# A diffusion layer with expert choice on one core: roots in batches and a new tail order, a column-tiled router, and the first attention unit moved into the gap

## The chip, the cores and the metric

One Trainium2 chip, one core of it. The metric is the device time of one launch in microseconds. The kernel before took 947.57 us, the median of three runs (947.54, 947.57, 952.59).

## The reference

One layer over 128 context tokens and 512 latent tokens of width 1024, all in float32. The attention sublayer has two groups of eight query heads with two key/value heads each (head size 64): group A global with normed and rotated queries and keys, group B windowed with a learned sink. Latents read their own keys and 128 cached context keys. Then comes a mixture of 16 experts by expert choice.

```python
def ffn_sublayer(x, shift, scale, gate, g_pre_ffn, ...):
    h = modulate(x, g_pre_ffn, shift, scale)           # rms_norm(x, g) * (1 + scale) + shift
    return x + gate * rms_norm(expert_choice_moe(h, ...), g_post_ffn)

def expert_choice_moe(h, w_router, w_gate, w_up, w_down):
    cap = 2 * T // 16                                  # 64 latent rows, 16 context rows per expert
    aff = softmax(einsum('btd,de->bte', h, w_router))
    g, idx = top_k(swapaxes(aff, 1, 2), cap)
    xg = h[idx]                                        # per expert
    y = (silu(xg @ w_gate) * (xg @ w_up)) @ w_down * g
    return zeros.at[idx].add(y)                        # for context and latents apart
```

Both kinds of token pass the same layer with their own modulation vectors. Outputs are both streams and the context's new keys and values.

## The kernel before, in words

The program is written out by hand for each engine, in its queue's order, with semaphores between engines. Tokens lie in five tiles of 128 (`TILES`): tile 0 is context, tiles 1 to 4 are latents.

**Projections.** `project(i)`, i = 0 to 14, makes columns for the five tiles three times (keys and values, then A's queries, then B's). ScalarE copies each result (`nat`), VectorE norms and rotates it (`rot`), TensorE turns it (`turn_qk(k)` is the tile of i = k - 1), ScalarE copies the high part (`high_part(k)`) and VectorE subtracts for the low part (`low_part(k)`). `rotate_last` and `turn_qk(15)` belong to the last tile, i = 14, and run among the first attention units.

**Attention.** 80 units (`HEAD_UNITS`) of one head and one tile, 40 of group A and then 40 of group B (`A_UNITS` = 40). Unit u passes `scores(u)` on TensorE, `maxima(u)` on VectorE (maximum and factor), `exponentials(u)` on ScalarE, normalisation on VectorE, `turn_probs(u)` on TensorE, `copy_pT(u)` on ScalarE, and for each pair `values` on TensorE and `attn_out` on VectorE. In iteration u TensorE does `turn_probs(u - 1)`, `scores(u + 2)`, values, and for B also the output projection of a tile that is ready, spread over the eight units of the next one. Behind it come, still inside the loop, the norm (roots on POOL), the residual `add_out`, the turn of x1 (`turn_x1`), and `route_logits(o)`: eight matmuls whose stationary side is the token tile and whose moving side is 16 columns of the router table `wrm`. `logits_of`, `exp_logits` and `affinities` make the softmax over experts. Tiles 3 and 4 are finished behind the loop, and VectorE selects rows for all experts (`top_eight`).

**Experts.** Eight slots of 2 MB hold weights; SP issues each load when its slot is free. Slots 0 to 5 are loaded for expert 0 when attention's buffers are free, slots 6 and 7 (over `reg2_qt`) with expert 1's gate weights when the normed rows are stored. POOL gathers rows by indirect DMA and scatters results by indirect DMA with addition. `product_c` is one slot's product for the context rows, `product_l` for the latents; both split the array in column groups of 32. `turn_rows_c`, `turn_rows_l` turn gathered rows; `keep_busy` issues matmuls whose result nobody reads. Expert 0 begins with its context products in front of `gate_l(0, 0)`, from where each expert follows the last.

**The end.** The sums over all experts but the last are read back and squared on ScalarE, gated (`gate_sum`), rooted on POOL (`root` is a power by -0.5) and added to x1 (`add_x1`), while the last expert still runs. Its rows are made apart: `add_last(n)` (n = 1 context, 0 latents), a squared sum over ScalarE, a matmul that merges partitions (line 1091, behind all expert products on TensorE), `mean_last`, a root, and `rows_last_c` in four parts or `rows_last_l`. POOL stores these rows by two indirect DMAs, the first behind the stores of all five tiles:

```python
            pool.wait_ge(stored, 16 * (4 + TILES))
            pool.wait_ge(f_ready, TILES + 4)
```

## Time and profile before

| | |
|---|---|
| time of the profiled execution | 948.19 us |
| its span, first to last instruction | 946.2 us |
| median of the three runs | 947.57 us |
| TensorE busy | 884.3 us (93%) |
| VectorE / ScalarE / POOL busy | 365.8 / 216.5 / 102.6 us |
| mean granted TensorE clock | 0.986 of full |
| moved by DMA | 269.31 MB, 285 GB/s over the span |

The page cuts the span into 40 slices of 23.7 us. Its DMA row stands at 9 in the first slices, falls to 0 during attention and is at 9 from slice 17 to the last but one; the row of TensorE is at 9 nearly throughout, so the shares of the whole span tell little. A timeline row gives the start, the time from its first to its last instruction, engine, line, operation, shapes, and in brackets the idle time before it with what ended it. A float32 matmul leaves two records, so 8 matmuls are x16. Windows give busy us of each engine in a stretch, with the number of instructions in brackets, the granted clock as a share of 2.4 GHz, DMA's share and its rate.

### The profile page before, as it was taken

To read this page: it belongs to the slowest core of one execution; us is meant where nothing else is said; L and a number is where in the kernel's file an instruction comes from. 1 tells how busy PE (TensorE), PEld (TensorE's weight loads), DVE (VectorE), ACT (ScalarE), POOL (GpSimd) and SP (SyncE) were. 2 spreads that over 40 slices of the span, in tenths; PEclk is the share of its full clock that TensorE was granted. 3 is DMA by queue.
4 is the path that set the end of the run, shared out by engine and by line. 5 is a ranking of instruction groups with operands and counts; after the bars stand their busy time and mean duration, and the time that the engine had idled before them with its cause. 6 is when DMAs were issued, how large, how long until landed. Compare 5 with 4: busy or idle time off the path is not lost. (4 is left out here: it accounts for less than half of the span.)

```text
span 946.2 us, 19909 instructions
## 1 busy us (share of the span) xinstructions
PE 884.3 (93%) x8641; PEld 442.2 (47%) x8641; DVE 365.8 (39%) x977; ACT 216.5 (23%) x528; POOL 102.6 (11%) x137
## 2 busy tenths in 40 slices
PE   3999998899899999779999999999999999999984
PEld 3544444777656665533444443443444443433431
DVE  4255635888766766811112021121113120210126
ACT  3132223666645653400000000000000000000012
POOL 2021200000000000100110111011101101110225
PEclk9999999999999999899999999999999999999998
DMA  9997532300001116969999999999999999999983
GB/s 337 351 367 279 212 144 96 122 2 1 2 1 46 45 46 239 414 242 405 398 396 411 397 398 403 404 397 397 411 397 397 396 410 398 398 407 391 359 321 151
DMA packets 77717, 269.31 MB, mean 285 GB/s; under 512 B 6208, under 2 KB 9984, under 8 KB 77632
## 3 DMA queue, kind: packets, MB, share of 16 engines
q1 hardware_dynamic: 72384, 251.42, 67.8%
q0 software_dynamic: 4160, 13.90, 5.1%
q10 hardware_dynamic: 1088, 2.74, 0.7%
q8 instruction: 68, 1.11, 0.5%
q14 instruction: 17, 0.14, 0.0%
HBM read 252.06 MB, written 15.99 MB: 283 GB/s over the span
## 5 line engine op out<-in xcount | busy, mean ns | idle before, releaser
L954 PE MATMUL ps<-ring,reg 128*32 128x512 f32 x1792 | 201.6, 592 | 0.0
L1812 DVE TENSOR_SCALAR mod<-ps,kt 64x512 f32<-64x512 f32 x30 | 22.5, 750 | 255.9 <-PE ps L954 255.7
L954 PEld LDWEIGHTS ps<-ring,reg 128*32 128x32 f32 x1792 | 59.1, 110 | 111.8 <-issue 103.3
L966 PE MATMUL ps<-ring,values_in 128*32 128x256 f32 x1536 | 93.6, 386 | 4.0 <-issue 2.9
L1325 ACT ACTIVATE reg<-ps 128x256 f32<-128x256 f32 x16 | 6.1, 384 | 366.6 <-PE ps L1006 354.1
L954 PE MATMUL ps<-ring,kt 128*32 128x512 f32 x768 | 86.8, 592 | 0.0
L809 PE MATMUL ps<-ring,reg 128*128 128x512 f32 x160 | 76.4, 604 | 0.0
L966 PEld LDWEIGHTS ps<-ring,values_in 128*32 128x32 f32 x1536 | 50.0, 112 | 54.1 <-issue 24.8
L655 PE MATMUL ps<-ring,reg_qt 128*128 128x512 f32 x160 | 70.6, 594 | 0.0
L966 PE MATMUL ps<-ring,reg 128*32 128x256 f32 x1024 | 60.9, 379 | 2.5 <-DMA ring<-in_w_down 1.9
L1269 ACT ACTIVATE ring<-ps 128x640 f32<-128x640 f32 (+3 forms) x80 | 44.4, 555 | 72.5 <-PE ps L738 69.9
L738 PE MATMUL ps<-ident,ring 128*128 128x128 f32 x288 | 47.7, 285 | 14.0 <-DVE ring L1676 7.7
L1971 POOL TENSOR_TENSOR small<-mhalf 128x1 f32<-128x1 f32 x31 | 9.5, 306 | 460.1 <-DVE kt L1815 426.7
L1175 ACT ACTIVATE ring<-ps,small 128x640 f32<-128x640 f32 (+3 forms) x80 | 51.0, 638 | 7.9 <-DVE small L1576 7.9
L738 PEld LDWEIGHTS ps<-ident,ring 128*128 128x128 f32 x288 | 33.8, 144 | 37.2 <-issue 19.0
L966 PEld LDWEIGHTS ps<-ring,reg 128*32 128x32 f32 x1024 | 33.0, 110 | 36.8 <-issue 12.9
L954 PEld LDWEIGHTS ps<-ring,kt 128*32 128x32 f32 x768 | 25.4, 110 | 46.8 <-issue 42.8
L655 PEld LDWEIGHTS ps<-ring,reg_qt 128*128 128x128 f32 x160 | 29.6, 190 | 34.7 <-issue 34.7
L760 PE MATMUL ps<-ring,values_in 128*64 128x128 f32 x576 | 40.3, 280 | 0.6 <-ACT ring L1269 0.6
L809 PEld LDWEIGHTS ps<-ring,reg 128*128 128x128 f32 x160 | 28.5, 189 | 24.7 <-issue 24.0
L1676 DVE TENSOR_SCALAR ring<-ring,small 128x640 f32<-128x640 f32 (+3 forms) x80 | 36.8, 460 | 2.8
L631 PE MATMUL ps<-ring,reg_qt 128*128 128x512 f32 x80 | 35.9, 596 | 1.3 <-ACT reg_qt L1122 1.3
(235 smaller groups left out, 1000.7 us busy)
## 6 DMA issues: line engine op xcount, KB each, us to landing
ring<-in_w_up SPq DMA_DIRECT2D x32, 2048.0 KB, 22.7
ring<-in_w_down SPq DMA_DIRECT2D x32, 2048.0 KB, 22.8
ring<-in_w_gate SPq DMA_DIRECT2D x16, 2048.0 KB, 21.6
reg_qt<-in_w_gate SPq DMA_DIRECT2D x16, 2048.0 KB, 22.9
ring<-in_w_ada SPq DMA_DIRECT2D x12, 2048.0 KB, 12.2
reg<-in_x_sample SPq DMA_DIRECT2D x8, 512.0 KB, 6.5
ring<-in_w_in SPq DMA_DIRECT2D x2, 2048.0 KB, 14.1
ring<-in_w_out SPq DMA_DIRECT2D x2, 2048.0 KB, 10.0
```

Source lines behind the costliest of these rows:

```text
L631: last = pe.matmul(projected(t), hT[:, c, t * P:(t + 1) * P], w[:, c, :], start=(c == 0), stop=(c == KC - 1))
L655: last = pe.matmul(projected(i), hT[:, c, t * P:(t + 1) * P], w[:, c, :], start=(c == 0), stop=(c == KC - 1))
L738: last = pe.transpose(two[2][:, b * P:(b + 1) * P], probs[:, u % 3, b * P:(b + 1) * P], ident[:, :])
L760: last = pe.matmul(ps[64 * hh:64 * hh + 64, bank, 0:P], v, pT[:, k % 2, hh, n * P:(n + 1) * P], start=(n == 0), stop=(n == len(blocks) - 1))
L809: last = pe.matmul(out_at(o)[:, n, :], attnT[:, c, t * P:(t + 1) * P], unit_at(wout_units[c // 4], 4)[:, c % 4, n * 512:(n + 1) * 512], st ...
L954: last = pe.matmul(o[64 * n + r:64 * n + r + 32, :], x(4 * hf + j, r), w[:, j, n * HALF:(n + 1) * HALF], start=(hf == 0 and j == 0), stop= ...
L966: last = pe.matmul(o[32 * q:32 * q + 32, :], x(c), w[:, j, q * QUART:(q + 1) * QUART], start=(c == 0), stop=(c == KC - 1))
L1175: act.activation(dst, scores_of(u), ACT.Exp, bias=negm[:, b:b + 1], scale=DH ** -0.5, accum_out=den[:, b:b + 1]).then_inc(exp_done, 1)
L1269: act.activation(pT[:, k % 2, u % 2, 0:n], two[2][:, 0:n], ACT.Copy).then_inc(pT_ready, 1)
L1676: dve.tensor_scalar(probs[:, u % 3, 0:n], probs[:, u % 3, 0:n], rden[:, b:b + 1], None, ALU.mult)\
L1812: dve.tensor_scalar(put_l[:, n * HALF:(n + 1) * HALF], ps[rows, 3, :], g_l[rows, e:e + 1], None, ALU.mult)
L1971: pool.tensor_tensor(held, mhalf[:, 0:1], mhalf[:, 1:2], ALU.add).then_inc(held_ops, 1)
```

## The change

**Router.** `route_logits` becomes `route_parts` and `route_merge`. In `route_parts` the table (now `wrm_by`, 32 columns a chunk, in a part of `kt` that is cleared first) is the stationary side and the tokens move, 128 columns, in four column groups. ScalarE copies the four partial sums (`copy_parts`), and one matmul with `merge`, a sum of four slices of the identity, adds them and turns them back. The logits of a tile are read one unit later. The table is made by VectorE at unit 44, where it was at unit 2.

**First unit.** `turn_qk(13)` goes ahead of `project(14)`, `high_part(13)` and `low_part(13)` with it, and unit 0's maxima, exponentials and normalisation stand beside that projection; `turn_probs(0)` and `scores(1)` come ahead of `turn_qk(14)`, whose high and low parts follow unit 1's exponentials and maxima. `rotate_last` moves from unit 0 to unit 1. The gates' gains move from unit 4 to unit 14.

**Between attention and experts.** `turn_aff(4)` goes ahead of `turn_rows_c(0)`, `turn_lists` behind `product_c(2)`, `turn_rows_l(0)` from ahead of the turn of context's activations to behind `product_c(4)`; there are more calls of `keep_busy`.

**End.** POOL makes the five roots in batches of 3 and 2. VectorE does all five `gate_sum` ahead of the additions, the additions stand among the last expert's rows in another order, and `rows_last_l` goes ahead of the four `rows_last_c`. POOL's first store waits for six rows ready instead of nine.

Three places show what moved. First VectorE around the first unit, before: `q_b<-ps` on line 1497 are low parts, 1569 and 1576 `maxima`, 1675 and 1676 the normalisation, 1484 begins a rotation.

```order
L1581 TENSOR_SCALAR small<-ps 16x2
L1497 TENSOR_TENSOR q_b<-ps,q_b 64x4x128 x2
L1584 TENSOR_SCALAR nsink<-sink 128x8
L1497 TENSOR_TENSOR q_b<-ps,q_b 64x4x128 x2
L1661 COPY rbias<-ps 128x32
L1569 TENSOR_REDUCE small<-ps 128x1
L1576 TENSOR_SCALAR small<-small 128x1
L1675 RECIPROCAL small<-small 128x1
L1676 TENSOR_SCALAR ring<-ring,small 128x640
L1484 TENSOR_TENSOR reg<-reg 128x512
L1487 TENSOR_TENSOR reg<-reg 128x16x16 x2
L1491 TENSOR_TENSOR reg<-reg 128x512
```

And with the change (low parts are line 1532, `maxima` 1554 and 1561, normalisation 1572 and 1573, rotation 1519):

```order
L1710 COPY rbias<-ps 128x32
L1554 TENSOR_REDUCE small<-ps 128x1
L1561 TENSOR_SCALAR small<-small 128x1
L1532 TENSOR_TENSOR q_b<-ps,q_b 64x4x128 x2
L1554 TENSOR_REDUCE small<-ps 128x1
L1561 TENSOR_SCALAR small<-small 128x1
L1572 RECIPROCAL small<-small 128x1
L1573 TENSOR_SCALAR ring<-ring,small 128x640
L1519 TENSOR_TENSOR reg<-reg 128x512
L1522 TENSOR_TENSOR reg<-reg 128x16x16 x2
L1526 TENSOR_TENSOR reg<-reg 128x512
```

The part of tile 14 has moved from ahead of `maxima(1)` to behind it, and the last rotation from behind the first normalisation to behind the second.

Second, TensorE at the start of the experts, before: line 966 is `product_c`, 933 `turn_rows_l`, 1062 the turn of context's activations, 954 `product_l`.

```order
L915 MATMUL ps<-ident,kt 128x16 x2
L966 MATMUL ps<-ring,values_in 32x256 x32
L966 MATMUL ps<-reg_qt,values_in 32x256 x16
L933 MATMUL ps<-ident,reg 128x128 x8
L1062 MATMUL ps<-ident,reg 128x128 x2
L966 MATMUL ps<-ring,reg 32x256 x32
L954 MATMUL ps<-ring,reg 32x512 x64
```

And with the change (`product_c` 984, `keep_busy` 916, `turn_rows_l` 951, activations' turn 1080, `product_l` 972):

```order
L933 MATMUL ps<-ident,kt 128x16 x2
L984 MATMUL ps<-ring,values_in 32x256 x16
L984 MATMUL ps<-reg_qt,values_in 32x256 x16
L916 MATMUL ps<-ident 128x128 x3
L1080 MATMUL ps<-ident,reg 128x128 x2
L984 MATMUL ps<-ring,reg 32x256 x16
L951 MATMUL ps<-ident,reg 128x128 x8
L984 MATMUL ps<-ring,reg 32x256 x16
L972 MATMUL ps<-ring,reg 32x512 x64
```

The turn of latents' rows now stands between the two down products, behind the turn of activations.

Third, VectorE's last rows before: line 1859 is `gate_sum`, 1864 `add_x1`, 1871 `add_last`, 1876 `gain_last`, 1880 `mean_last`, 1887 `rows_last_c`, 1893 `rows_last_l`.

```order
L1859 TENSOR_TENSOR ring<-reg_qt 128x1024
L1864 SCALAR_TENSOR_TENSOR ring<-ring,small,reg 128x1024
L1871 SCALAR_TENSOR_TENSOR reg_qt<-ps,kt,reg 128x256
L1864 SCALAR_TENSOR_TENSOR ring<-ring,small,reg 128x1024
L1876 TENSOR_TENSOR reg_qt<-reg_qt,reg 128x256
L1880 TENSOR_SCALAR small<-ps 128x1
L1871 SCALAR_TENSOR_TENSOR reg_qt<-ps,kt,reg 128x512
L1876 TENSOR_TENSOR reg_qt<-reg_qt,reg 128x512
L1887 SCALAR_TENSOR_TENSOR kt<-reg_qt,small,reg 16x256
L1880 TENSOR_SCALAR small<-ps 128x1
L1887 SCALAR_TENSOR_TENSOR kt<-reg_qt,small,reg 16x256 x2
L1893 SCALAR_TENSOR_TENSOR reg_qt<-reg_qt,small,reg 128x512
```

And with the change (`gate_sum` 1907, `add_x1` 1912, `add_last` 1919, `gain_last` 1924, `mean_last` 1928, `rows_last_l` 1941, `rows_last_c` 1935):

```order
L1907 TENSOR_TENSOR ring<-reg_qt 128x1024 x4
L1912 SCALAR_TENSOR_TENSOR ring<-ring,small,reg 128x1024
L1919 SCALAR_TENSOR_TENSOR reg_qt<-ps,kt,reg 128x256
L1924 TENSOR_TENSOR reg_qt<-reg_qt,reg 128x256
L1912 SCALAR_TENSOR_TENSOR ring<-ring,small,reg 128x1024
L1928 TENSOR_SCALAR small<-ps 128x1
L1912 SCALAR_TENSOR_TENSOR ring<-ring,small,reg 128x1024 x2
L1919 SCALAR_TENSOR_TENSOR reg_qt<-ps,kt,reg 128x512
L1912 SCALAR_TENSOR_TENSOR ring<-ring,small,reg 128x1024
L1924 TENSOR_TENSOR reg_qt<-reg_qt,reg 128x512
L1928 TENSOR_SCALAR small<-ps 128x1
L1941 SCALAR_TENSOR_TENSOR reg_qt<-reg_qt,small,reg 128x512
```

`mean_last` of the context (the first of line 1928) has moved from behind all five additions to ahead of three of them.

The diff, cut:

```diff
@@ TensorE @@
+                if i == 3 * TILES - 2:
                     scores(0)
+                    turn_qk(3 * TILES - 2)
+            turn_probs(0)
+            scores(1)
             turn_qk(3 * TILES - 1)
             spread_shift()
-            scores(1)
...
-            def route_logits(o):
+            def route_parts(o):
...
                 for c in range(KC):
                     if c % 4 == 0:
                         pe.wait_ge(h2_ready, 2 * o + (1 + c // 4 if o == TILES - 1 else 2))
-                    last = pe.matmul(dst, h2T[:, c, t * P:(t + 1) * P],
-                                     wrm[:, (KC * cond + c) * E:(KC * cond + c + 1) * E], start=(c == 0),
-                                     stop=(c == KC - 1))
+                    q = c % 4
+                    last = pe.matmul(bank[32 * q:32 * q + 32, 0:P], wrm_by[:, cond, c, :], h2T[:, c, t * P:(t + 1) * P],
+                                     start=(c < 4), stop=(c >= 4))
+                last.then_inc(parts_done, 1)
+            def route_merge(o):
+                bank = (out_at(o) if o < TILES - 1 else out_at(o - 1))[:, 1, :]
+                pe.wait_ge(parts_copied, o + 1)
+                pe.matmul(bank[:, P:P + E], logit_parts, merge, start=True, stop=True).then_inc(router_done, 1)
...
                 if o >= 2 and j == 7:
-                    route_logits(o - 2)
+                    route_parts(o - 2)
+                if o >= 3 and j == 1:
+                    route_merge(o - 3)
...
-            keep_busy(3, 4)
-            turn_lists()
             pe.wait_ge(silu_done, 1)
             weight_in(2, 0)
             product_c(2, GC[:, QUART:], context_of(0))
+            keep_busy(3, 4)
+            turn_lists()
             weight_in(3, 0)
             product_c(3, GC[:, QUART:], context_of(0))
             gate_in(0, 0, 1)
             product_c(SLOTS, GC[:, 0:QUART], context_of(1)).then_inc(up_c, 1)
-            pe.wait_ge(xc_ready, 2)
-            turn_rows_l(0)
+            keep_busy(3, 3)
             pe.wait_ge(act_c_ready, 1)
...
             product_c(4, YC[:, 0:QUART], acts_c)
+            pe.wait_ge(xc_ready, 2)
+            turn_rows_l(0)
@@ ScalarE @@
+            def copy_parts(o):
+                bank = (out_at(o) if o < TILES - 1 else out_at(o - 1))[:, 1, :]
+                act.wait_ge(parts_done, o + 1)
+                if o:
+                    act.wait_ge(router_done, o)
+                act.activation(logit_parts, bank[:, 0:P], ACT.Copy).then_inc(parts_copied, 1)
...
+            copy_pT(0)
             for u in range(n_units):
-                if u:
+                if u >= 2:
                     copy_pT(u - 1)
                 if u + 1 < n_units:
                     exponentials(u + 1)
+                if u == 0:
+                    high_part(3 * TILES - 1)
...
             square_x1_half(1)
+            copy_parts(4)
             normalise_x1(4)
@@ VectorE @@
+                if i == 3 * TILES - 2:
+                    maxima(0)
                 if i >= 1:
                     low_part(i - 1)
+                if i == 3 * TILES - 2:
+                    low_part(i)
+                    normalise(0)
...
-                if u == 0:
-                    rotate_last()
+                if u:
+                    normalise(u)
+                if u == 0:
+                    low_part(3 * TILES - 1)
+                if u == 1:
+                    rotate_last()
...
+                if u == A_UNITS + 4:
+                    dve.wait_ge(scores_done, A_UNITS)
+                    link(dve.memset(kt[:, 2048:2048 + 2 * KC * CPAD], 0.0))
...
             for t in range(1, TILES):
                 gate_sum(t)
-                add_x1(t - 1)
+            add_x1(0)
             add_last(1)
-            add_x1(TILES - 1)
             gain_last(1)
+            add_x1(1)
             mean_last(1)
+            add_x1(2)
+            add_x1(3)
             add_last(0)
+            add_x1(4)
             gain_last(0)
-            rows_last_c(0)
             mean_last(0)
-            rows_last_c(1)
-            rows_last_c(2)
             rows_last_l()
-            rows_last_c(3)
+            for q in range(4):
+                rows_last_c(q)
@@ POOL @@
-            for t in range(TILES):
-                pool.wait_ge(f_squared, t + 1)
-                pool.tensor_scalar(msf[:, t:t + 1], ssf[:, t:t + 1], EPS, None, ALU.add).then_inc(f_mean, 1)
-                root(rsf[:, t:t + 1], msf[:, t:t + 1], 1, f_mean, f_rstd, t + 1)
+            for k, (a, b) in enumerate(((0, 3), (3, TILES))):
+                pool.wait_ge(f_squared, b)
+                pool.tensor_scalar(msf[:, a:b], ssf[:, a:b], EPS, None, ALU.add).then_inc(f_mean, 1)
+                root(rsf[:, a:b], msf[:, a:b], b - a, f_mean, f_rstd, k + 1)
...
-            pool.wait_ge(f_ready, TILES + 4)
+            pool.wait_ge(f_ready, TILES + 1)
```

## Rows read from the trace of the kernel before

**Rows 1.** Busy time by stretches of 5 us: stretch, length, engines, granted clock, DMA, GB/s.

```profile
405.00:410.00 5.00, 2.22 (x44) 1.05 (x34) 0.00 (x0) 0.00 (x0) 0.40 (x1) 1.00 1.02 411
```

**Rows 2.** Timeline of SP's DMA issues at 355 to 425, and one's landing time.

```profile
362.48 0.93 SPq L476 DMA_DIRECT2D ring<-in_w_gate  x2
...
394.09 2.07 SPq L476 DMA_DIRECT2D reg_qt<-in_w_gate  x2
...
reg_qt<-in_w_gate SPq DMA_DIRECT2D x2, 2048.0 KB, 17.4
```

**Rows 3.** Timeline of TensorE, start of the experts: start, us, operation [idle before].

```profile
411.58 3.41 PE L966 MATMUL ps<-reg_qt,values_in 128*32 128x256 f32 x32 [4.36 <-DMA reg_qt<-in_w_gate]
...
414.92 1.09 PE L933 MATMUL ps<-ident,reg 128*128 128x128 f32 x8
...
416.80 3.66 PE L966 MATMUL ps<-ring,reg 128*32 128x256 f32 x64 [0.56 <-ACT reg L1325]
...
420.25 13.94 PE L954 MATMUL ps<-ring,reg 128*32 128x512 f32 x128
```

**Rows 4.** First attention unit: TensorE, the clock by stretches, ScalarE, VectorE.

```profile
159.23 1.43 PE L704 MATMUL ps<-k_a,q_a 128*128 128x320 f32 x8
...
164.51 1.33 PE L738 MATMUL ps<-ident,ring 128*128 128x128 f32 x5 [3.84 <-DVE ring L1676]
...
165.49 1.41 PE L704 MATMUL ps<-k_a,q_a 128*128 128x320 f32 x4
...
166.71 1.05 PE L673 MATMUL ps<-ident,reg 128*128 128x128 f32 x4
...
162.00:164.00 2.00, 0.00 (x0) 0.00 (x0) 1.90 (x6) 0.17 (x1) 0.00 (x0) 0.51 0.99 371
...
158.42 2.40 ACT L1155 ACTIVATE q_b<-ps 64x512 fp32r<-64x512 f32 x4
...
163.83 0.80 ACT L1175 ACTIVATE ring<-ps,small 128x640 f32<-128x640 f32 x1 [3.01 <-DVE small L1576]
...
159.63 1.39 DVE L1497 TENSOR_TENSOR q_b<-ps,q_b 64x512 fp32r<-64x512 f32 x2 [3.32 <-ACT q_b L1155]
...
162.79 0.81 DVE L1569 TENSOR_REDUCE small<-ps 128x1 f32<-128x640 f32 x1
...
164.37 0.68 DVE L1484 TENSOR_TENSOR reg<-reg 128x512 f32<-128x512 f32 x1
...
166.37 0.82 DVE L1569 TENSOR_REDUCE small<-ps 128x1 f32<-128x640 f32 x1
```

**Rows 5.** TensorE around a router in the timeline, and groups of line 560.

```profile
332.81 1.85 PE L838 MATMUL ps<-wrm,reg 128*128 128x16 f32 x16
...
334.52 0.64 PE L738 MATMUL ps<-ident,ring 128*128 128x128 f32 x4
...
L560 PE MATMUL ps<-ring,reg 128*32 128x128 f32 x256 | 8.0, 277 | 1.4 <-DMA ring<-in_w_ada 1.4
...
L560 PEld LDWEIGHTS ps<-ring,reg 128*32 128x32 f32 x256 | 6.9, 112 | 2.6 <-issue 2.5
```

**Rows 6.** The router table on VectorE, and TensorE at unit 47, timelines.

```profile
169.53 0.48 DVE L1684 SCALAR_TENSOR_TENSOR wrm<-wr,colmod 128x128 f32<-128x128 f32 x2
...
254.21 0.33 PE L738 MATMUL ps<-ident,ring 128*128 128x128 f32 x1 [0.64 <-DVE ring L1676]
```

**Rows 7.** Timeline of the tail, TensorE, VectorE, POOL; landing of the last stores.

```profile
925.23 7.05 PE L954 MATMUL ps<-ring,reg 128*32 128x512 f32 x64
...
933.15 1.28 DVE L1864 SCALAR_TENSOR_TENSOR ring<-ring,small,reg 128x1024 f32<-128x1024 f32 x1 [0.37 <-POOL small L1923]
...
934.76 0.74 DVE L1871 SCALAR_TENSOR_TENSOR reg_qt<-ps,kt,reg 128x512 f32<-128x512 f32 x1
...
938.85 0.44 POOL L1971 TENSOR_TENSOR small<-mhalf 128x1 f32<-128x1 f32 x1 [1.33 <-issue]
...
out<-ring SPq DMA_DIRECT2D x1, 512.0 KB, 2.7
```

More of the change, by code:

```diff
@@ L706, in scores, with turn_probs @@
                 last.then_inc(scores_done, 1)
+            def turn_probs(u):
+                g, h, t = HEAD_UNITS[u]
+                pe.wait_ge(probs_ready, u + 1)
+                if u == 0:
+                    pe.wait_ge(mod_ready, N_MOD + 2)
+                    pe.wait_ge(qkT_ready, 3 * TILES - 1)
+                    pe.wait_ge(qkT_act, 3 * TILES - 1)
+                if u:
+                    pe.wait_ge(pT_ready, u)
+                for b in range(key_count(g, t) // P):
+                    last = pe.transpose(two[2][:, b * P:(b + 1) * P], probs[:, u % 3, b * P:(b + 1) * P], ident[:, :])
+                last.then_inc(probs_turned, 1)
             for i in range(3 * TILES):
@@ L907, in _ @@
                 cast_gate(1, r)
-            route_logits(4)
+            route_parts(4)
+            route_merge(4)
             turn_aff(3)
```

149 lines of the change are left out of this document (75 added, 74 removed).

## The prediction

> **What bounds the kernel now.** I read the page first: TensorE is busy nearly all the span, and DMA stands near its ceiling from slice 17 on. Two engines near full say little about a change that touches the joints, so I went on to the table by stretches and to the timelines of each engine, to find in each stage the wait that ends last.
>
> Stage one, projections and attention, to 362 us. In the second half of attention TensorE runs with hardly a gap; that half is its own work. The gap to see is at the first attention unit: TensorE ends two scores at 160.66 and starts the first turn of probabilities at 164.51, after 3.84 us of waiting for VectorE, and the granted clock falls meanwhile to 0.51, near its lower level of 1.2 GHz [rows 4].
>
> Stage two, 362 to 420 us. The loads of the first expert start at 362.48, right behind the last attention unit. DMA is full from there to about 414: between 405 and 410, for one, its share is 1.02 at 411 GB/s, while TensorE is busy for 2.22 of the 5 us [rows 1]. SP issues the gate weights of expert 1 (slots 6 and 7) at 394.09, and they take 17.4 us to land, where 2 MB at 411 GB/s are 5.1 us: the rest is queue [rows 2]. TensorE waits 4.36 us for slot 6 and resumes at 411.58 [rows 3]. So this stage is as long as its bytes: it starts when attention ends, and what the selection on VectorE or the router on TensorE saves behind 362 is slack.
>
> Stage three, the experts: TensorE from `gate_l(0, 0)` at 420.25 on [rows 3], and everything else is released by it. It moves rigidly with 420.25.
>
> Stage four, the tail. The last expert's products end at 925.23 + 7.05 = 932.28. `add_last(0)`, the sum of the last expert's latents, starts only at 934.76, and POOL begins the final store at 938.85 [rows 7].
>
> The span is 946.2 us, the profiled run 948.19 (2.0 around it), the median of the three runs 947.57. I sum differences on the profiled execution and add them to the median. A measurement tells about 1%, 9.5 us, from no change; that is the bound of my three classes.
>
> **The change, part by part.**
>
> *Router.* Each `route_logits` is 8 matmuls with 16 moving columns (16 records): 332.81 to 334.52 = 1.71 us of TensorE [rows 5]. `route_parts` has weights of 32 columns and 128 moving ones, four column groups in turn. The same shape stands in the first modulation products: 256 records in 8.0 us busy, 0.031 each, so 16 x 0.031 = 0.5 us [rows 5]. The merge is one matmul like those removed, 1.71 / 8 = 0.21. Three routers stand ahead of the last attention unit, two merges do: 3 x (1.71 - 0.5) - 2 x 0.21 = 3.2 us saved where TensorE is the bound. Bounds: 3.2, and -0.6 if the small products are no cheaper (below). ScalarE's new copies and VectorE's logits, one unit later, have gaps in that half and cost nothing; should that cover fail, the price is the copy, some 0.3 us each.
> Here the Trainium skill speaks against the change. "TensorE: Matmul & The Clock Gate", Part 3 (packing small matmuls), says that a weight load overlaps matmuls in flight only where the row group differs; these four share their rows. By that rule nearly nothing would be saved. The row of before disagrees: its loads take 0.112 us each, and yet a record comes every 0.031 [rows 5]. The sum by the rule would stand 3.8 us higher; I go by the row.
>
> *First unit.* TensorE now turns key/query tile 13 ahead of `project(14)` and unit 0's softmax runs beside that projection: the 3.84 us wait goes. What is late next? ScalarE's `high_part(14)` now stands behind `exponentials(1)`; VectorE's `low_part(14)` waits for it ahead of `maxima(2)`; and `turn_qk(15)`, at its old place in TensorE's queue, needs `rotate_last`, which VectorE now reaches only after `maxima(2)` and `normalise(1)`. Followed by durations: with tile 13's turn first (0.44), scores 1 ends about 159.8 and the bias is spread at 160.8; `maxima(1)` (0.81 and its small factor, 0.9) to 161.8, its exponentials (0.80 and the read of their sum, 0.9) to 162.7, `high_part(14)` (half of 2.40) to 163.9, `low_part(14)` (1.39) to 165.4, `maxima(2)` and `normalise(1)` (162.79 to 164.37 for the first pair, 1.6) to 167.0, rotation (164.37 to 166.37, 2.0) to 169.0 [rows 4]. So `turn_qk(15)` runs at 169.0 where it ran at 166.71 [rows 4], with `turn_probs(1)` and all later turns behind it; TensorE stands 5.4 us ahead of it (163.6 to 169.0) instead of 3.84. Carrying on through units 2 to 5, the saved first normalisation, router table and gains (some 1.7 us of VectorE) win back most: by unit 5 TensorE is 0.9 later than before. That is at the full clock. Before, the clock fell in such a gap, and the scores at 165.49 took till 166.71, 1.22, where two at the full clock took 1.43 at 159.23 [rows 4]; a longer gap should leave about 3 us of the work behind it at half rate, 1.0 more. I take +1.9. Bounds: -1.5 (the wait's 3.84 less the 2.3 by which the rotation is later) and +3.0.
>
> *VectorE's new set-up at unit 44.* The router table moves from the first units, and gets a memset and three small sums. A memset of 512 columns is at most a sum of that width (0.68) [rows 4], the three small sums some 0.2 each with their links, the two products 0.48 [rows 6]: 1.5 to 1.8 us. There TensorE waits for VectorE already (0.64 at 254.21) [rows 6], and only behind that come output projections as a cushion. VectorE has some 0.5 to 0.7 of slack, so +1.0; bounds 0 and +1.8. The gate's gains, two products of half that width, move to unit 14, where VectorE has short pauses in each pair of units: +0.1, at most their 0.7.
>
> *End of attention:* -3.2 + 1.9 + 1.0 + 0.1 = -0.2. The loads start 0.2 earlier and so does slot 6's landing. ScalarE now copies `parts(4)` ahead of normalising the last tile: its store, and SP's issue behind it at 394.09, come some 1.6 later. The queue covers this: of slot 6's 17.4 us some 12 were spent behind others [rows 2]. Uncovered it would cost up to 1.6.
>
> *Start of the experts.* `turn_lists`, `keep_busy` and the context's products change places in the 5 us that TensorE waits for slot 6: nothing. Behind slot 6 the turn of latents' rows (1.09, some 0.9 of the queue's time) moves from ahead of the turn of context's activations to behind `product_c(4)`. Before: 414.92, turns, a wait of 0.56, two products, `gate_l(0, 0)` at 420.25, so a product is (420.25 - 416.80) / 2 = 1.7 [rows 3]. After: three busy matmuls to 415.6, turn 0.4, copy 0.55, `product_c(4)` to 418.3, rows to 419.2, `product_c(5)` to 420.9: +0.7. The 0.9 no longer covers VectorE's product of context's activations. Bounds 0 and +1.1.
>
> *Tail.* The roots in two batches take POOL off the path. But VectorE's queue is now: five gates, addition 0, context's last rows, addition 1, `mean_last(1)`, additions 2 and 3, `add_last(0)`. `mean_last(1)` waits for a matmul that TensorE has behind all expert products, so before 932.1 it can't run; additions 2 and 3, ready by then, wait with VectorE idle from about 930.7. Then 1.28 each, some 1.2 back to back, so `add_last(0)` starts at 934.6 against 934.76: the same [rows 7]. Behind it now stands addition 4 ahead of `gain_last(0)` (+1.2), in front of context's four rows (-1.5). Latents' row ready at 938.7; but POOL's final store also waits for the last tile's store, issued at 936.6 and landing 2.7 later, 939.3 [rows 7]. POOL starts at 939.4 instead of 938.85: +0.6. Bounds -1.5 (VectorE free for `add_last(0)` at 932.3, a store that lands in time) and +1.6 (the landing 1 us slower).
>
> *Sum:* -0.2 + 0.7 + 0.6 = +1.1 us. 947.57 + 1.1 = 948.7.
>
> **The rivals.**
> 1. *The gaps close as meant.* The first unit gains its 1.5, the table at unit 44 is hidden, the router gives 3.2: attention ends 4.7 earlier; with +0.7 and 0 at the tail -4.0: 943.6. For it: VectorE stood idle 3.32 us before 159.63 and now works there [rows 4]; against: `rotate_last` is behind two more units. 0.25.
> 2. *The small products are no cheaper.* If each of the 16 loads of 0.112 is paid one after another, that is 1.8 like the 1.71 now; the router saves nothing and pays two merges, 3.8 on my sum: 952.5. Against it is the pace of the modulation products [rows 5]. 0.05. This is what the rule of the Trainium skill named above would make here.
> 3. *Slower at the first unit.* TensorE's gap ahead of `turn_qk(15)` decides once the rotation ends past 169: each later microsecond is one of the loop's, and the half clock lasts over units 1 to 4. Price +3.0 there instead of 1.9 and 1.8 at unit 44 instead of 1.0: 1.9 on my sum, 950.6, slower than before. For it: the clock at 0.51 [rows 4]. 0.2.
> 4. *The slots' loads come too late.* If the queue were dry when SP issues at 395.7, 1.6 more: 950.3. Against it: the 12 us of queue [rows 2]. 0.03.
>
> **How the numbers follow.** Forecast 948.7 with 0.45 (0.02 is for what none of these names), the rivals as above. Its own range, ±1.5. The range for 8 in 10 takes in most of rival 1 and rival 3 with half of their spread: 943.8 to 951.5. None of the mechanisms has a price near 9.5 us; I leave 0.02 for faster and 0.02 for slower by over 1% for what I haven't seen, and 0.96 for within.
>
> **What would show it.** Right: `turn_qk(15)` near 169 with a gap of over 5 us before it and half clock behind; router products of 0.5 us; TensorE's first `gate_l` at 420 to 421.5; VectorE idle until TensorE's last product ends, then two additions ahead of the latents' row; the final store at 939 to 940 less the shift. Wrong: the loads of expert 0 issued before 360 or after 364.5, DMA below 0.9 between 365 and 410, slot 6 landing later than 49.5 us behind the first load, or POOL waiting for a root in the tail.

## The result, and the profile after

The changed kernel took 955.46 us (median of 6 runs), the one of before 948.68 beside it: ratio 1.006, 95% interval 1.0031 to 1.0088. A second set gave 956.03 against 949.19, ratio 1.007 (1.0051 to 1.009). So it is some 6 us slower. The forecast was 948.7, +1.1, in a range of 943.8 to 951.5: the direction was right, the size and the range were wrong. All times and ratios are of fast executions; one execution of before_tail_mended below, of 2837 us, is the only one left out as slow.

The page of the changed kernel, its span, busy times and clock:

```profile
span 954.0 us, 20012 instructions
...
PE 888.1 (93%) x8689; PEld 442.3 (46%) x8689; DVE 366.9 (38%) x981; ACT 217.0 (23%) x533; POOL 98.6 (10%) x131
...
PEclk9999999799999999989999999999999999999997
```

Shares say nothing again; slice 8 of the clock (167 to 191 us) does, a 7 where before has a 9. The first unit, timeline of the changed kernel (start, us, operation, idle before it), answering to [rows 4]:

```profile
164.45 0.85 PE L706 MATMUL ps<-k_a,q_a 128*128 128x320 f32 x4 [1.41 <-ACT ring L1195]
170.65 1.12 PE L675 MATMUL ps<-ident,reg 128*128 128x128 f32 x4 [5.36 <-DVE reg L1526]
171.56 1.28 PE L720 MATMUL ps<-ident,ring 128*128 128x128 f32 x5
...
164.29 1.18 ACT L1175 ACTIVATE q_b<-ps 64x512 fp32r<-64x512 f32 x2
...
165.51 1.39 DVE L1532 TENSOR_TENSOR q_b<-ps,q_b 64x512 fp32r<-64x512 f32 x2 [2.03 <-ACT q_b L1175]
166.93 0.82 DVE L1554 TENSOR_REDUCE small<-ps 128x1 f32<-128x640 f32 x1
168.51 0.69 DVE L1519 TENSOR_TENSOR reg<-reg 128x512 f32<-128x512 f32 x1
```

The gap is 5.36 us where it was 3.84, and it ends with the rotation. The same kernel by stretches (length; busy TensorE, weight loads, VectorE, ScalarE, POOL; granted clock; DMA share; GB/s):

```profile
165.00:170.00 5.00, 0.29 (x3) 0.03 (x1) 4.34 (x10) 1.36 (x3) 0.00 (x0) 0.64 0.55 194
170.00:175.00 5.00, 4.35 (x19) 4.16 (x20) 3.13 (x8) 2.12 (x5) 0.00 (x0) 0.50 0.00 0
...
410.00:415.00 5.00, 0.57 (x8) 0.34 (x12) 0.00 (x0) 0.00 (x0) 0.00 (x0) 0.72 1.03 419
415.00:420.00 5.00, 4.63 (x40) 2.44 (x32) 0.42 (x1) 0.33 (x1) 0.00 (x0) 0.60 0.47 189
...
925.00:930.00 5.00, 3.96 (x40) 2.14 (x44) 2.62 (x4) 2.42 (x6) 0.00 (x0) 0.76 0.99 372
```

At three places (170, 415 and 925 us) TensorE's work behind a wait runs with the clock at 0.5, its level of 1.2 GHz, for all or a part of the stretch: the means are 0.50, 0.60 and 0.76. Slot 6's stretch had such a fall before, too, a shorter one:

```profile
410.00:415.00 5.00, 3.42 (x33) 1.46 (x34) 0.00 (x0) 0.00 (x0) 0.00 (x0) 0.66 0.89 356
415.00:420.00 5.00, 4.43 (x70) 3.38 (x74) 3.10 (x5) 0.38 (x1) 1.15 (x2) 1.00 0.25 59
```

A router, a merge and the new set-up at unit 44, timeline (answers to [rows 5, 6]):

```profile
309.39 0.64 PE L844 MATMUL ps<-reg,kt 128*32 128x128 f32 x16
309.96 0.66 PE L720 MATMUL ps<-ident,ring 128*128 128x128 f32 x4
...
316.47 0.29 PE L852 MATMUL ps<-cvec,gqk 128*128 128x16 f32 x2
...
253.65 0.48 DVE L1727 MEMSET kt<- 128x512 f32 x1
```

The small products take 0.57 us to the next operation, where a router took 1.71. The start of the experts (answers to [rows 2, 3]):

```profile
365.23 1.57 SPq L478 DMA_DIRECT2D ring<-in_w_gate  x2
...
414.43 3.64 PE L984 MATMUL ps<-reg_qt,values_in 128*32 128x256 f32 x32 [6.39 <-DMA reg_qt<-in_w_gate]
420.20 1.93 PE L984 MATMUL ps<-ring,reg 128*32 128x256 f32 x32 [0.57 <-ACT reg L1360]
422.06 1.09 PE L951 MATMUL ps<-ident,reg 128*128 128x128 f32 x8
...
424.83 2.75 PE L972 MATMUL ps<-ring,reg 128*32 128x512 f32 x23
```

(The last row is cut off at 427 us by its view.) The loads start 2.75 later than in [rows 2], past the prediction's own mark of 364.5 for being wrong; slot 6 is used 2.85 later, and the first `gate_l` starts 4.58 later. The last expert and the tail (answers to [rows 7]):

```profile
924.15 1.23 DVE L1907 TENSOR_TENSOR ring<-reg_qt 128x1024 f32<-128x1024 f32 x1 [12.00 <-DMA reg_qt<-sum_c]
...
925.88 0.44 PE L1024 MATMUL ps<-ident,reg 128*128 128x128 f32 x2 [2.25 <-DVE reg L1839]
927.06 5.35 PE L984 MATMUL ps<-ring,reg 128*32 128x256 f32 x64
932.23 7.05 PE L972 MATMUL ps<-ring,reg 128*32 128x512 f32 x64
...
939.63 0.16 DVE L1928 TENSOR_SCALAR small<-ps 128x1 f32<-128x1 f32 x1 [1.42 <-PE ps L1111]
939.71 2.48 DVE L1912 SCALAR_TENSOR_TENSOR ring<-ring,small,reg 128x1024 f32<-128x1024 f32 x2
942.11 0.74 DVE L1919 SCALAR_TENSOR_TENSOR reg_qt<-ps,kt,reg 128x512 f32<-128x512 f32 x1
...
946.76 0.31 POOL L2020 TENSOR_TENSOR small<-mhalf 128x1 f32<-128x1 f32 x1 [1.42 <-DMA out<-ring]
```

Before, the wait ahead of the last down products was 1.71 us, and the first of them took 3.66 instead of 5.35:

```profile
920.56 0.44 PE L1006 MATMUL ps<-ident,reg 128*128 128x128 f32 x2 [1.71 <-DVE reg L1791]
921.16 0.66 PE L1011 MATMUL ps<-ident,reg 128*128 128x128 f32 x4 [0.16 <-DVE reg L1796]
921.75 3.66 PE L966 MATMUL ps<-ring,reg 128*32 128x256 f32 x64
```

TensorE ends at 939.28, 7.0 later than before; VectorE stands idle 1.42 us at `mean_last(1)` with two additions queued behind it; POOL's final store waits for the last tile's store. This execution against the one of before, in its 7.8 us of span: 1.4 ahead of unit 0, 3.0 over the first unit, 0.8 at unit 44, -2.4 by the routers, 0.1 to slot 6, 1.7 to `gate_l(0, 0)`, 2.4 to TensorE's last product, 0.7 behind it.

### The profile page after: what moved, and what is told of

Its sections match the earlier page's. It is cut to its first block and busy times, and to the rows that moved or that the text cites. A ratio compares the mean times of both kernels' runs of the same rounds, so it can differ in the third digit from the quotient of the medians.

```text
span 954.0 us, 20012 instructions
## 1 busy us (share of the span) xinstructions
PE 888.1 (93%) x8689; PEld 442.3 (46%) x8689; DVE 366.9 (38%) x981; ACT 217.0 (23%) x533; POOL 98.6 (10%) x131
## 5 line engine op out<-in xcount | busy, mean ns | idle before, releaser
L657 PE MATMUL ps<-ring,reg_qt 128*128 128x512 f32 x160 | 70.6, 595 | 0.0
L984 PE MATMUL ps<-reg_qt,values_in 128*32 128x256 f32 x512 | 32.5, 397 | 6.4 <-DMA reg_qt<-in_w_gate 6.4
```

The lines of the kernel that those rows point to most:

```text
L657: last = pe.matmul(projected(i), hT[:, c, t * P:(t + 1) * P], w[:, c, :], start=(c == 0), stop=(c == KC - 1))
L984: last = pe.matmul(o[32 * q:32 * q + 32, :], x(c), w[:, j, q * QUART:(q + 1) * QUART], start=(c == 0), stop=(c == KC - 1))
```

## The experiments

Differences in us are (ratio - 1) times the median of before in the same set, with the 95% interval; the changed kernel stands at +5.7 (2.9 to 8.3) and +6.6 (4.8 to 8.5), 6.2 as their mean. "Gained" is 6.2 less a run's figure. By the intervals of both (an estimate) it is good to some 2 us, so the times alone show only the gains of 3.0 and more; smaller ones rest on their traces, of one execution each. Edits are against the changed kernel where nothing else is said.

**after_again** (nothing edited)

> The changed kernel once more, nothing edited. Its first profile lies 7.9 us of span above the one of before: 1.4 arose ahead of the first unit (half clock at 23 to 27 us), 3.0 over the first unit, 0.7 at unit 44, -2.4 with the routers, 1.7 between slot 6 and gate_l(0, 0), 2.2 at the wait ahead of the last expert's down products and the half clock behind it, 0.7 in the tail. Theory A, the orders cause all of it: the new profile shows each of these again, span 953 to 955, the median 6 to 7 above before. Theory B, the half clock at the start (1.4) and ahead of the last products (1.7 of the 2.2) are chance of one execution: they are missing in the new profile, span 950 to 951, and the median is 4 to 5 above before.

+6.6. Its profile has the clock's fall at the start and the one at the last expert again (wait 2.33), and one more, at 255 to 262. Span and time are theory A's, yet the list of falls differs between two executions of one kernel.

**undo_first_unit**

```diff
-                    turn_qk(3 * TILES - 2)
-            turn_probs(0)
-            scores(1)
             turn_qk(3 * TILES - 1)
             spread_shift()
+            scores(1)
```

(with ScalarE's and VectorE's order of before likewise)

> The changed kernel with the order of the first unit put back on TensorE, ScalarE and VectorE. Theory: the new order costs 3.0 (by unit 8 the softmax runs 4.4 later than before, 1.4 of it from the start), so this kernel is 3.0 faster than the changed one, with the 3.8 us gap of before ahead of turn_probs(0), and the normalisation of unit 8 within 0.3 of before relative to the first projections. Rival, the delay is covered later by the queue of expert weights (the loads start earlier but slot 6 lands when it did): the loads are issued 3 earlier and the time stays within 1 us of the changed kernel.

+3.0 (1.8 to 4.3): 3.2 less than the changed kernel. The loads are issued at 362.56. The theory held.

**gate_behind**

```diff
-            gate_sum(0)
             activations(E - 1)
+            gate_sum(0)
```

(and `square_sum(0)` behind the two copies)

> The changed kernel with the first gate_sum of the tail moved behind the last expert's activations on VectorE, and the first square_sum behind the copies of the turned activations on ScalarE. Theory: TensorE's 2.25 us wait ahead of the last expert's down products stands because VectorE holds the activations behind a gate that waits 12.0 us for the context sums' load; with it gone TensorE waits under 0.6 there, keeps the full clock (1.7 us) and the kernel is 2.5 to 3.5 faster than the changed one. Rival, the up products end as late as the gate, so that the activations can't start sooner: less than 0.5 faster, the wait still 1.7 to 2.3.

+3.2 (2.1 to 4.4), 3.0 gained. The timeline of this kernel:

```profile
921.79 0.69 DVE L1844 TENSOR_TENSOR reg<-reg,ps 128x512 f32<-128x512 f32 x1 [3.08 <-PE ps L972]
...
922.53 0.66 PE L1029 MATMUL ps<-ident,reg 128*128 128x128 f32 x4 [0.50 <-DVE reg L1844]
```

The activations now wait for their products, and TensorE 0.50. The gate ahead of them, which both kernels have, was what held them.

**undo_tail** (roots one at a time, VectorE's order of before)

```diff
-            for k, (a, b) in enumerate(((0, 3), (3, TILES))):
+            for t in range(TILES):
```

> The changed kernel with the tail of before (roots one at a time, each addition behind its gate, context's rows ahead of latents'). Theory: the tail alone costs 0.7, measured from TensorE's last expert product to the final store (7.3 before, 8.0 after), so 0.5 to 1 faster than the changed one, and the wait ahead of the last down products stays (1.7 to 2.3). Rival, the batches also delay the last expert: the wait there falls under 1.7 and the kernel is 2 to 3 faster.

+5.1 (3.3 to 6.8), 1.1 gained; the wait stays at 2.18. From TensorE's last expert product to the final store it has 7.36, the changed one 7.97. Theory, within what it resolves.

**undo_start** (order of before from the context's first products to `gate_l(0, 0)`, the new fillers taken out; a part of the edit)

```diff
+            pe.wait_ge(xc_ready, 2)
+            turn_rows_l(0)
...
             product_c(4, YC[:, 0:QUART], acts_c)
-            pe.wait_ge(xc_ready, 2)
-            turn_rows_l(0)
```

> The changed kernel with the order of before at the experts' start, from the context's first products to gate_l(0, 0) (the turn of latents' rows ahead of product_c(4), the lists turned behind turn_rows_c(1), no filler ahead of the turned activations). In the changed one gate_l(0, 0) starts 9.9 to 10.4 behind slot 6 (9.9 where the clock was full by 416), before 8.67. Theory: the turn of the rows (1.02 of the queue) now stands in the open, and the kernel is 1.2 to 1.7 faster than the changed one (956.0), with gate_l(0, 0) 8.7 to 9.2 behind slot 6. Rival, the difference is the half clock behind slot 6 alone: gate_l(0, 0) stays 9.7 or more behind slot 6 and the time within 0.5 of the changed one.

+4.0 (2.3 to 5.7), 2.2 gained; `gate_l(0, 0)` 8.05 behind slot 6, earlier than the theory's 8.7 to 9.2. More than the 1.02 of the rows' turn: in this execution the clock was full from slot 6 to `gate_l(0, 0)`.

**table_later**

```diff
-                if u == A_UNITS + 4:
+                if u == A_UNITS + 12:
```

> The changed kernel with VectorE's set-up for the router (memset, folded identity, two products) at unit 52 instead of unit 44, where VectorE waits 0.5 to 1.4 for TensorE's scores. Theory: at unit 44 it costs 0.75 by itself, and by the longer wait of TensorE it brings on a half clock at 255 to 262 in some executions (two of five profiles whole, one in part), so 0.75 to 2 faster than the changed one (956.0), and no clock under full between 250 and 265. Rival, half clock there comes of the short units themselves: it is seen again, and only up to 0.75 is gained.

+5.3 (3.7 to 7.0), 0.9 gained. VectorE's normalisations are late by the same amount at units 44 and 56 (3.16), so the set-up is hidden. The clock at 255 to 260, first the changed kernel's second execution, then this one:

```profile
255.00:260.00 5.00, 4.50 (x14) 2.87 (x15) 4.58 (x20) 3.33 (x14) 0.00 (x0) 0.56 0.01 3
```

```profile
255.00:260.00 5.00, 4.04 (x18) 2.10 (x17) 4.65 (x18) 2.95 (x12) 0.00 (x0) 1.00 0.00 0
```

**rotate_later**

```diff
-                if u == 1:
+                if u == 2:
                     rotate_last()
```

(and the parts 14 and 15 and `turn_qk(15)` one unit later)

> The changed kernel with the rest of the first unit's work one unit later on all three engines: high_part(14) and low_part(14) behind unit 1, rotate_last behind unit 2, turn_qk(15) behind turn_probs(1), high_part(15) and low_part(15) another unit on. Theory: what costs 3.0 at the first unit is that turn_probs(1) stands behind turn_qk(15), which waits for rotate_last; here normalise(1) ends about 165.1 instead of 168.6, TensorE's gap of 5.35 shrinks to under 2, and the kernel is 3 to 6 faster than the changed one (956.0). Rival, VectorE's work is only put off and units 2 to 5 wait for it instead: unit 8 is normalised as late as before the edit within 1.5, and the kernel is under 1.5 faster.

+8.0 (6.6 to 9.3). TensorE still waits 4.20 for the rotation, at 170.25. In its profile the first unit costs 0.8 less than in the changed kernel, in the times nothing is gained. The profile is of the fastest of its six executions (953.83 us, the median is 956.42), and what the others lost is not shown. The theory of a gain fell.

**mean_later**

```diff
-            mean_last(1)
             add_x1(2)
             add_x1(3)
+            mean_last(1)
```

> The changed kernel with mean_last(1) moved behind the additions 2 and 3 on VectorE. Theory of the prediction: VectorE sits idle (1.42 us) ahead of mean_last(1) until TensorE's last product ends, with two additions ready behind it; so add_last(0) starts 1.4 earlier, the final store too, and the kernel is 1.2 to 1.6 faster than the changed one (956.0). Rival, the final store is released by the last tile's store or by context's root, which now comes later: under 0.4 faster.

+5.0 (3.1 to 6.9), 1.2 gained. Its timeline: the sum of the last latents starts right behind TensorE's end (940.06), and the tail takes 5.6 instead of 8.0, 2.4 less where the theory had 1.4: the last tile's store, which gates the final one, comes earlier too.

```profile
940.49 0.75 DVE L1919 SCALAR_TENSOR_TENSOR reg_qt<-ps,kt,reg 128x512 f32<-128x512 f32 x1
```

**router_alone** (the diffs of undo_first_unit, undo_start and undo_tail together)

> The changed kernel with the first unit, the experts' start and the tail all put back: what is left of the change is the router in parts, its table at unit 44 and the gate's gains at unit 14. Theory: three routers give 2.4 ahead of the loads, the table takes 0.75, or up to 3.5 where the clock falls at 255: 0 to 2 faster than before, middle 1.3; the loads of expert 0 issued at 360.5 to 363. Rival, the small products and what stands around them bring nothing in the end (the gain is lost at the slots' loads): the loads are issued 1.5 or more earlier, slot 6 lands as before, the time is within 0.5 of before.

-1.3 (-2.8 to 0.0). Loads issued at 361.13, 1.35 earlier than in [rows 2]. The interval reaches 0, but the trace has the gain: the router in parts is the one piece of the change that pays.

**all_mended** (router with the table at unit 52; first unit and start of before; `gate_behind`; and in the tail)

```diff
-            mean_last(1)
             add_x1(2)
             add_x1(3)
+            add_x1(4)
+            mean_last(1)
             add_last(0)
-            add_x1(4)
```

> Router in parts with its table at unit 52; first unit and experts' start as before; roots in two batches, but with the first gate and square behind the last expert's activations, and all five additions ahead of mean_last(1). Theory, a sum: -2.4 for the routers, -1.2 and the risk of a half clock for the wait of 1.71 ahead of the last down products, -2.3 in the tail (1.65 as with mean_last later, against before, and 0.9 more because the last tile's store is issued earlier): 942 to 944.5 where before is 948.5 to 949. Rival, TensorE is held there by something else next (the loads of the slots, the turned activations) and the final store by a root: 945.5 or above.

945.46, -4.2 (-5.8 to -2.5): faster than both kernels. Timeline:

```profile
919.95 7.05 PE L969 MATMUL ps<-ring,reg 128*32 128x512 f32 x64
...
930.38 0.73 DVE L1907 SCALAR_TENSOR_TENSOR reg_qt<-ps,kt,reg 128x512 f32<-128x512 f32 x1
```

TensorE ends at 927.0, and the last sum starts 3.4 later, behind VectorE's additions: VectorE is the tail's bound now, and takes back part of what the wait gave. The time is the one that my rival gave; what holds it is not what the rival named, a root or TensorE's next wait.

**before_tail_mended** (the changed tail with the diffs of gate_behind and all_mended, on the kernel of before)

> The kernel of before with the tail alone changed: roots in two batches, first gate and square behind the last expert's activations, all five additions ahead of mean_last(1). Theory: -1.2 at the wait and -2.3 in the tail, so 3 to 4.5 faster than before, and the difference from the kernel with the router in parts, all mended, is the router's 2.4. Rival, without the batches' own cost there is nothing to gain in the tail: under 1.5 faster.

-0.7 (-2.1 to 0.7), the rival: TensorE ends at 930.94, the last sum starts at 933.94.

**before_again**

> The kernel of before once more, for a second profile. In the first, TensorE waited 1.71 ahead of the last expert's down products and the clock stayed full; in the changed one it waited 2.25 to 2.47 and the clock fell for 3 to 4 us in four of five profiles. Theory A, the wait's length decides: full clock there again, wait 1.6 to 1.9, and none at 23 to 27 or 255. Theory B, it falls by chance: half clock behind a wait as short as 1.71.

-0.2 (-1.6 to 1.2), as it should be. The wait was 2.02, longer than either theory had it, and yet the products behind it took their 3.66 at the full clock, which fits neither; all profiles together settle it below.

```profile
919.08 0.44 PE L1006 MATMUL ps<-ident,reg 128*128 128x128 f32 x2 [2.02 <-DVE reg L1791]
...
920.26 3.66 PE L966 MATMUL ps<-ring,reg 128*32 128x256 f32 x64
```

**rotate_early**

```diff
                 if u == 0:
-                    low_part(3 * TILES - 1)
-                if u == 1:
                     rotate_last()
+                    low_part(3 * TILES - 1)
```

> The changed kernel with rotate_last ahead of low_part(14) on VectorE, in unit 0 as before, and all else as changed. Theory of the prediction: what is late is the rotation behind maxima(2) and normalise(1). Here it ends about 2 us behind maxima(1), so that turn_qk(15) runs at 165.5 to 167 where it ran at 170.3 to 171, the 5.35 us gap splits in two of 3 at most, and the kernel is 1.5 to 3 faster than the changed one (956.0 where before is 949.2). Rival, VectorE's work from its first maxima on is the chain, in whatever order (moving the rotation the other way gained nothing): unit 8 is normalised within 0.7 of the changed kernel, and the time stays within 1.

+4.5 (2.8 to 6.2), 1.7 gained; timeline:

```profile
164.14 1.11 PE L675 MATMUL ps<-ident,reg 128*128 128x128 f32 x4 [0.27 <-DVE reg L1526]
...
167.26 1.33 PE L720 MATMUL ps<-ident,ring 128*128 128x128 f32 x5 [2.01 <-DVE ring L1573]
```

The gap of 5.36 is split in 0.27 and 2.01, `turn_qk(15)` runs at 164.14 (the theory had 165.5 to 167), and units 7 to 44 run 0.4 ahead of before, instead of 2.4 to 3.0 behind. The theory held: it is the rotation's place.

**start_alone** (the diff of undo_start reversed, on the kernel of before)

> The kernel of before with the changed order at the experts' start alone. Theory: the turn of latents' rows (1.02) is in the open, and gate_l(0, 0) comes 9.9 to 10.4 behind slot 6 instead of 8.67: 1.2 to 1.7 slower than before. Rival: what the put-back order gained (2.2 to 3 by the medians) was of the kernel it stood in; alone it costs under 0.6.

+1.8 (0.4 to 3.3). `gate_l(0, 0)` comes 10.85 behind slot 6.

**rows_ahead**

```diff
-            keep_busy(3, 3)
+            pe.wait_ge(xc_ready, 2)
+            turn_rows_l(0)
             pe.wait_ge(act_c_ready, 1)
```

> The changed kernel with turn_rows_l(0) alone moved back ahead of the turned activations, in place of the filler of three; the rest of the new order at the experts' start stays. Theory: that one move is what the start costs (1.02 of TensorE's queue), so 1 to 1.5 faster than the changed one, gate_l(0, 0) 8.9 to 9.4 behind slot 6. Rival: the turned rows wait for their gather (0.4 to 0.8 in three profiles with that order), or the fillers and the lists' turn matter too: under 0.6 faster.

+5.0 (3.1 to 6.9), 1.2 gained; `gate_l(0, 0)` 9.52 behind slot 6, 10.40 in the changed one and 10.5 on average in ten profiles with the new start. That is the theory's size, 0.1 past its range, and the rows are not the whole of the 2.2.

**tail_alone** (the diff of undo_tail reversed, on the kernel of before)

> The kernel of before with the changed tail alone. Theory: from TensorE's last expert product to the final store 8.0 instead of 7.3, the wait ahead of the last down products as before (1.7 to 2.0): 0.4 to 1.3 slower than before. Rival: the tail's half microsecond is covered by what the wait and the clock do in each execution: within 0.3.

+1.8 (0.5 to 3.1); 7.97 from the last product to the final store against 7.31, and the clock fell behind a wait of 1.65.

**no_fillers**

```diff
-            keep_busy(3, 6)
             turn_aff(4)
             turn_rows_c(0)
-            keep_busy(3, 10)
```

> The changed kernel without the 16 fillers ahead of the context's first products (keep_busy(3, 6) and keep_busy(3, 10)); the rest of the new start stays. In ten profiles with the new order the clock stayed full from 380 to 408 and fell for some 7 us at the wait for slot 6, over the products behind it; with the old order it fell at 386 to 392 already. Theory: the fillers keep the clock where DMA sets the pace and it is worth nothing, and the fall comes where it costs; without them it falls at 388 to 400, gate_l(0, 0) stands 57 to 58.8 behind the first load instead of 59.5, and the kernel is 0.7 to 1.5 faster than the changed one (6.8 above before). Rival: the fall behind slot 6 comes of the 6 us wait itself: it is there again whole, gate_l(0, 0) 59 or more behind, the time within 0.5.

+3.9 (2.2 to 5.6), 2.3 gained. By stretches, this kernel:

```profile
395.00:400.00 5.00, 1.96 (x21) 1.15 (x24) 4.73 (x19) 4.18 (x9) 1.29 (x2) 0.50 1.03 415
...
415.00:420.00 5.00, 4.43 (x60) 2.57 (x52) 0.42 (x1) 0.38 (x1) 0.00 (x0) 0.88 0.51 206
```

The clock is low from 392 to 402, where DMA is full anyway, and again for 2.9 us behind slot 6, where ten profiles with the fillers have 3.6 to 5.9. `gate_l(0, 0)` stands 57.4 behind the first load. Of the 2.2 that this is less than their mean, 0.8 lie behind slot 6; the other 1.3 lie ahead of it, since slot 6 came 47.7 behind the first load, and that varies by 2.5 us in either order.

**mended_early_rotation** (all mended, and the changed first unit with the rotation early)

> The kernel with all mended (945.5 where before was 949.7), and with the changed first unit in it after all, but rotate_last in unit 0 ahead of low_part(14). With that order the softmax of units 7 to 44 ran 0.45 ahead of before in its one profile, where the changed order ran 2.6 to 4.4 behind and the old one 0.2 off. Theory: 0.3 to 1 faster than all mended, 4.5 to 5.5 faster than before. Rival, in the medians the changed first unit still costs what the half clock behind its first waits takes: 0.5 or more slower than all mended (under 3.7 faster than before).

944.82, -4.7 (-6.6 to -2.9): the fastest, though not told apart from all mended at -4.2.

## Why the prediction was wrong, step by step

| step | forecast | by the trace | by the times |
|---|---|---|---|
| routers; table at unit 44; gains | -2.1 | -1.6 | -1.3 alone |
| first unit | +1.9 | +2.9 | +3.2 (undone) |
| start of the experts | +0.7 | +2.1 | +1.8 alone, 2.2 undone |
| tail | +0.6 | +0.7 | +1.8 alone, 1.1 undone |
| sum | +1.1 | +4.1 | 5.5, of 6.2 |

The 7.8 us by which the changed kernel's first profile is longer hold 1.4 at the start of the program and 2.4 behind `gate_l(0, 0)` besides; the prediction had no term for either.

*Routers: mechanism right.* 16 records in 0.57 us (0.5 forecast), a merge 0.14 (0.21). The sum was 2.4 instead of 3.2: in the trace TensorE is 1.04 ahead at the next turn behind each router, and of the 0.36 that it loses behind each merge 0.16 are a longer wait for VectorE (0.38 us for 0.22). The rule of the Trainium skill ("TensorE: Matmul & The Clock Gate", Part 3) that loads of one row group do not overlap would have left nothing; the trace disagrees, with loads of 0.11 us and a product every 0.04.

*First unit: chain right, term mis-sized.* The late rotation, the 5.4 us gap (5.36) and `turn_qk(15)` at 169.0 (170.65, 1.4 of it from the start of the program) came as worked out. The step that failed is the winning back: "by unit 5 TensorE is 0.9 later than before", with 1.0 more for the clock. Over nine profiles with the changed order the softmax of unit 44 stands 2.4 to 3.0 later than in the first profile of before, once the lateness that each had at 149 us is taken off; in eight with the old order it stands 0.4 earlier to 0.1 later. The means are 2.9 apart. VectorE's saved 1.7 us won back nothing. Against before, and with the same lateness taken off, the turn of unit 1's probabilities on TensorE is 2.1 later in all nine, and that of unit 5's 2.4 to 3.0. router_alone tells why: there VectorE has the same set-up less in front of unit 5, its normalisation of that unit is 0.7 earlier, and TensorE's turns stand where they stood. Unit 5's turn, before, changed and router_alone:

```profile
177.52 0.77 PE L738 MATMUL ps<-ident,ring 128*128 128x128 f32 x5
...
181.92 0.77 PE L720 MATMUL ps<-ident,ring 128*128 128x128 f32 x5
...
177.79 0.77 PE L719 MATMUL ps<-ident,ring 128*128 128x128 f32 x5
```

Of these 1.4 and 0.3 are from the start of the program, which leaves 3.0 and none. The rest goes with the clock: it was low for 6.8 us in the two profiles with 2.4 and for 10.2 in the seven with 2.5 to 3.0 (in the changed kernel till 176.7, where before had 168.9). rotate_early shows by its trace that the place of the rotation decides.

*Unit 44: right size, and a risk left out.* The set-up costs 0.76 in each profile (+1.0 forecast). But in 6 of 12 profiles with it there, the clock fell at 252 to 262 and took 1.8 to 2.6 more by unit 56, in a seventh 1.5. In eight with the table earlier or later it never did.

*Start of the experts: the step that failed most.* I counted the rows' turn and let the rest stand in a wait. Measured from the first load of expert 0, `gate_l(0, 0)` starts 59.5 later on average in ten profiles with the new start (58.9 to 59.9), 57.4 in eight with the old (55.9 to 58.8): 2.1 for the 0.7 forecast. Slot 6 itself came nearly as forecast, 47.4 to 49.9 behind the first load in all 20 profiles, 0.4 later on average with the new start; the other 1.7 lie behind it (10.5 for 8.8). The turn of the rows in the open is 1.0 of them, where I had 0.7: 9.5 in rows_ahead. The rest goes with the clock, at an edit that I costed at nothing, the new fillers ahead of the context's first products and the work moved "in the 5 us that TensorE waits for slot 6: nothing". With the old order the clock falls at 385 to 393 in all eight, and TensorE then waits 1.0 to 4.8 us for slot 6. With the new one it stays full till 407 to 413, TensorE waits 5.6 to 6.7 us, and the clock falls in that wait in all ten, so that products behind it, on the path, run at half rate. With the old order the clock was low behind slot 6 in four of eight, before's first profile among them. Without the 16 fillers 9.65 us lie between slot 6 and `gate_l(0, 0)`, 0.8 less, the rows' turn still where the change put it. These 0.8 are one execution's; the 2.3 that the times gained there have an uncertainty as large, so the fillers' full share is not settled.

*Tail: right.* VectorE idle till TensorE's end, two additions ahead of the latents' row, the final store gated by the last tile's store: all as forecast, 0.7 for 0.6 in the trace; the times give 1.1 to 1.8, with intervals that take in both. mean_later shows by its trace (5.6 for 8.0) that the place of `mean_last(1)` was the price.

*The last expert's wait: no term, and open.* The fall behind the last expert's wait is 1.7 of the 2.4 there. The wait exceeded 1.6 us in 16 profiles, and the clock fell in 9 of them: at 1.65, 1.85 and 1.86, but not at 2.11, 2.18 or 2.54, so its length alone does not decide. In the four where it was under 0.9 it never fell. All nine have the new tail (of eleven that have it and the wait); in the five with the tail of before (before, before_again, router_alone, start_alone, undo_tail) it never fell, at waits of 1.71 to 2.54. The new tail leaves TensorE's own order as it was, and one execution each does not tell chance from an effect of the tail. Over all executions, the share of the clock not granted, times the span, is 15.5 us in tail_alone and 14.2 in before beside it, which speaks for an effect; so does its +1.8 where the trace's tail costs 0.7. The cure is the same: remove the wait (gate_behind).

*What stays unexplained.* The 1.4 us at the start of the program (clock down at 23 to 27 in after, after_again, undo_start, mean_later) lie in code that the change does not touch; no run explains them. Of the 6.2 us some 0.7 stay unassigned, within the intervals.

## What to carry to other kernels

A wait of TensorE costs its length, and what the clock then takes from the work behind it: a wait that ends ahead of path-bound work can be dear, the same fall inside a DMA-bound stretch was free here (no_fillers, 392 to 402), so fillers belong only where the work behind them is on the path. Time saved on an engine gains nothing if the next one in the chain does not wait for it (0.7 us of VectorE at unit 5 gave TensorE none). When work is pulled forward on one in-order engine, look at what it is pulled ahead of (here a rotation that TensorE's next turn needs, and a gate ahead of the last activations), and move that first. Batching a step (POOL's roots) saves nothing if the new order of its consumer idles at someone else's semaphore, as VectorE did for 1.42 us at `mean_last(1)`.

## What the runs showed that I had not expected

One program's executions differ in where the clock falls: the changed kernel's two profiles have three falls in common between the first unit and the tail, and one at 255 in the second only, worth 1.9 us. Waits of under 0.9 us ahead of the last products never brought a fall in four profiles; at units 45 to 48, four waits of 0.3 to 0.7 us in a row with little work between came with a fall in seven of twelve profiles; the eight without the set-up there have three such waits and no fall.
